# A depthwise convolution shared between VectorE and GpSimd: half the channels for each

## The reference

```python
def conformer_conv(a, g, conv_w, conv_b, ln_g, ln_b):
    z = a * jax.nn.sigmoid(g)                       # 256 tokens x 256 channels
    z = lax.conv_general_dilated(z, conv_w[:, None, :], window_strides=(1,),
                                 padding=[(D_CONV - 1, 0)],          # D_CONV = 31, causal
                                 dimension_numbers=('NWC', 'WIO', 'NWC'),
                                 feature_group_count=D_WIDTH) + conv_b
    return jax.nn.silu(layernorm(z, ln_g, ln_b))
```

## Time and profile before

| | |
|---|---|
| median of 3 runs | 1017.18 us (1016.47 to 1017.36) |
| the profiled execution | 1017.16 us, of which the span of the profile is 1015.3 us |
| busy: PE matmul, PE weight load | 1002.2 us (99%), 846.9 us (83%) |
| busy: DVE, ACT, POOL | 811.8 us (80%), 649.9 us (64%), 38.4 us (4%) |
| granted TensorE clock | full in all but the last instants |
| DMA | 257.13 MB, 253 GB/s over the span |

### The profile page before, as it was taken

One profiled execution on the slowest core, in us unless ns is written; L12 is line 12 of the kernel. 1 busy time (PEld: TensorE's weight loads), 2 busy tenths in 40 slices (PEclk: granted clock), 3 DMA queues, 4 the chain that ended last, 5 costly groups with the idle time before them and its releaser, 6 DMA issues.

```text
span 1015.3 us, 13999 instructions
## 1 busy us (share of the span) xinstructions
PE 1002.2 (99%) x4930; PEld 846.9 (83%) x4930; DVE 811.8 (80%) x1112; ACT 649.9 (64%) x890; POOL 38.4 (4%) x87
## 2 busy tenths in 40 slices
PE   7999999999999999999999999999999999999998
PEld 6888888888888888888888888888888988898887
DVE  5799888765544455699889768999889989989898
ACT  6658655555534443756674548787778787868775
POOL 6000000040000000100000000000000000000020
PEclk9999999999999999999999999999999999999999
DMA  9735555677555554844555556999999999999995
GB/s 272 240 122 168 172 179 168 209 241 248 169 195 188 195 177 129 289 147 133 178 172 181 189 190 217 323 379 389 365 340 393 384 364 346 390 369 362 358 395 204
DMA packets 117701, 257.13 MB, mean 253 GB/s; under 512 B 5217, under 2 KB 29859, under 8 KB 117649
## 3 DMA queue, kind: packets, MB, share of 16 engines
q1 hardware_dynamic: 113344, 243.55, 68.8%
q0 software_dynamic: 3296, 9.22, 3.3%
q10 hardware_dynamic: 1008, 3.67, 0.9%
HBM read 249.08 MB, written 7.34 MB: 253 GB/s over the span
## 4 chain that ended last, share of the span: by engine, by line
PE 89%; DVE 5%; ACT 3%; DMA 2%; issue 1%; SPq 0%; DVEq 0%; ACTq 0%
PE bank L390 27%; PE bank L392 27%; PE bank L391 27%; DMA ring<-in_w_in 2%; DVE wlo L378 1%; ACT whi L371 1%; PE bank L1082 1%; DVE dacc L1719 1%; PE bank L1005 1%; PE bank L1004 1%; PE bank L674 1%; DMA ring<-in_moe_w_gate 1%; PE bank L664 1%; PE bank L908 0%; PE bank L689 0%
## 5 line engine op out<-in xcount | busy, mean ns | idle before, releaser
L378 DVE TENSOR_TENSOR wlo<-ring,whi 128x1024 fp32r<-128x1024 f32 (+2 forms) x506 | 541.4, 1122 | 102.2 <-ACT whi L371 99.9
L371 ACT CAST whi<-ring 128x1024 fp32r<-128x1024 f32 (+2 forms) x506 | 463.4, 971 | 97.0 <-PE bank L392 79.1
L390 PE MATMUL bank<-whi,hTh 128*128 128x512 f32 (+3 forms) x992 | 375.4, 378 | 2.0 <-DVE wlo L378 1.3
L392 PE MATMUL bank<-whi,hTl 128*128 128x512 f32 (+3 forms) x992 | 370.4, 373 | 0.0
L391 PE MATMUL bank<-wlo,hTh 128*128 128x512 f32 (+3 forms) x992 | 370.1, 373 | 0.0
L390 PEld LDWEIGHTS bank<-whi,hTh 128*128 128x128 f32 x992 | 186.4, 188 | 32.4 <-issue 2.7
L392 PEld LDWEIGHTS bank<-whi,hTl 128*128 128x128 f32 x992 | 186.3, 188 | 29.1
L391 PEld LDWEIGHTS bank<-wlo,hTh 128*128 128x128 f32 x992 | 186.5, 188 | 28.4 <-issue 0.5
L390 PE MATMUL bank<-whi,oTh 128*128 128x512 f32 x392 | 155.4, 396 | 0.0
L392 PE MATMUL bank<-whi,oTl 128*128 128x512 f32 x392 | 153.1, 391 | 0.0
L391 PE MATMUL bank<-wlo,oTh 128*128 128x512 f32 x392 | 152.9, 390 | 0.0
(11 more groups left out here) (333 smaller groups left out, 672.4 us busy)
## 6 DMA issues: line engine op xcount, KB each, us to landing
ring<-in_w_in SPq DMA_DIRECT2D x40, 1024.0 KB, 5.2
ring<-in_moe_w_down SPq DMA_DIRECT2D x40, 1024.0 KB, 7.5
ring<-in_moe_w_gate SPq DMA_DIRECT2D x32, 1024.0 KB, 7.3
ring<-in_moe_w_up SPq DMA_DIRECT2D x32, 1024.0 KB, 8.2
ring<-in_moe_w_gate SPq DMA_DIRECT2D x16, 768.0 KB
ring<-in_moe_w_up SPq DMA_DIRECT2D x16, 768.0 KB, 7.4
ring<-in_ffn_w_gate SPq DMA_DIRECT2D x11, 1024.0 KB, 5.1
ring<-in_ffn_w_up SPq DMA_DIRECT2D x11, 1024.0 KB, 5.2
```

Source lines behind the costliest of these rows:

```text
L371: nc.scalar.copy(whi[pc.part(hf)][:, 0:n], pc.raw[:, hf * n:(hf + 1) * n]).then_inc(hi_done, 1)
L378: nc.vector.tensor_tensor(wlo[q][:, 0:n], pc.raw[:, hf * n:(hf + 1) * n], whi[q][:, 0:n].bitcast(F32), ALU.subtract).then_inc(lo_done, 1)
L390: nc.tensor.matmul(o, sh, wh, start=start, stop=False)
L392: return nc.tensor.matmul(o, sl, wh, start=False, stop=stop)
```

## The change

Of the two channel groups, group 1 moves to GpSimd. There each tap is two instructions, since the fused one isn't used: a product of the shifted view with the weight column into one of two temporaries (in `wsr`, which is free by then), and an addition to `dacc[:, 1]`. That is 1 + 30 x 2 = 61 instructions a layer. Each addition waits for its product and for the addition before. The call `conv(0)` stands behind `load_gain(1)` in GpSimd's program, `conv(1)` behind `load_gain(3)` and ahead of the filling of `yrows`.

DVE keeps group 0: 31 tap instructions a layer, each of which now waits for the one before (`link`). They are dealt anew to the steps: 4 in step 4, 4 in 6, 2 in 13, 3 in 14, 4 in 15, 5 in 16, 5 in 20, 4 in 22. After the last, DVE waits for `conv_done` from GpSimd and adds both groups.

```diff
+            def conv(l):
+                tmp = [wsr[:, 2 * i:2 * i + 2, :].rearrange("p g t -> p (g t)") for i in range(2)]
+                o, done = dacc[:, 1, :], (D_CONV - 1) * l
+                pool.wait_ge(zpad_ready, l + 1)
+                pool.wait_ge(wprep_ev, l + 1)
+                pool.wait_ge(param_in, 16 * N_PARAM * (l + 1))
+                nc.gpsimd.tensor_scalar(o, zpad[:, 1, 0:T], cw[:, 1, 0:1], dcol[:, 0, 1:2], ALU.mult,
+                                        ALU.add).then_inc(tap_sum, 1)
+                for j in range(1, D_CONV):
+                    nc.gpsimd.tensor_scalar(tmp[j % 2], zpad[:, 1, j:j + T], cw[:, 1, j:j + 1], None,
+                                            ALU.mult).then_inc(tap_product, 1)
+                    pool.wait_ge(tap_product, done + j)
+                    pool.wait_ge(tap_sum, D_CONV * l + j)
+                    nc.gpsimd.tensor_tensor(o, o, tmp[j % 2], ALU.add).then_inc(tap_sum, 1)
+                pool.wait_ge(tap_sum, D_CONV * (l + 1))
+                pool.engine_nop().then_inc(conv_done, 1)
...
             load_gain(1)
+            conv(0)
             pool.wait_ge(layer_done, 1)
             load_params(1)
             load_gain(2)
             load_gain(3)
+            conv(1)
...
-                for i in range(first, first + n):
-                    j, c = i // 2, i % 2
-                    if j:
-                        dve.wait_ge(dve_seq, own[0] - 1)
-                    z = zpad[:, c, j:j + T]
+                for j in range(first, first + n):
+                    z = zpad[:, 0, j:j + T]
                     if j == 0:
-                        ins = V.tensor_scalar(dacc[:, c, :], z, cw[:, c, 0:1], dcol[:, 0, c:c + 1], ALU.mult, ALU.add)
+                        ins = V.tensor_scalar(dacc[:, 0, :], z, cw[:, 0, 0:1], dcol[:, 0, 0:1], ALU.mult, ALU.add)
                     else:
-                        ins = V.scalar_tensor_tensor(out=dacc[:, c, :], in0=z, scalar=cw[:, c, j:j + 1],
-                                                     in1=dacc[:, c, :], op0=ALU.mult, op1=ALU.add)
-                    own[0] += 1
-                    ins.then_inc(dve_seq, 1)
-                if first + n == 2 * D_CONV:
-                    dve.wait_ge(dve_seq, own[0])
+                        ins = V.scalar_tensor_tensor(out=dacc[:, 0, :], in0=z, scalar=cw[:, 0, j:j + 1],
+                                                     in1=dacc[:, 0, :], op0=ALU.mult, op1=ALU.add)
+                    link(ins)
+                if first + n == D_CONV:
+                    dve.wait_ge(conv_done, l + 1)
                     V.tensor_tensor(dsum, dacc[:, 0, :], dacc[:, 1, :], ALU.add).then_inc(conv_ready, 1)
...
-                taps = {4: (0, 4), 5: (4, 10), 6: (14, 12), 13: (26, 4), 14: (30, 4), 16: (34, 8), 20: (42, 4),
-                        22: (46, 8), 23: (54, 8)}
+                taps = {4: (0, 4), 6: (4, 4), 13: (8, 2), 14: (10, 3), 15: (13, 4), 16: (17, 5), 20: (22, 5),
+                        22: (27, 4)}
```

More of the change, by code:

```diff
@@ L315, in build_trunk @@
         az_mm, az_ev = sem("az_mm"), sem("az_ev")
+        tap_product, tap_sum, conv_done = sem("tap_product"), sem("tap_sum"), sem("conv_done")
         conv_ready, dmean_mm, dsq_ready, dvar_mm, dms_root = (
```

## The result

| | before | changed |
|---|---|---|
| median | 1017.05 us (1016.47 to 1017.36) | 1031.9 us (1031.07 to 1032.86) |
| span of the profiled execution | 1015.3 us | 1030.0 us |

The ratio is 1.0146, with a 95% interval of 1.0134 to 1.0159: the changed kernel is 14.85 us slower. The prediction was 1029.5 us.

What follows compares the result with a forecast made beforehand. TensorE's matmuls, busy 1002.2 of 1015.3 us, were taken as the bound, with DVE a near second. Collisions of 6.8 us in layer 0 and 5.4 in layer 1, 12.2 together, gave 1029.4, predicted as 1029.5 us, range 1015.9 to 1043.

Steps and rivals of the forecast that it cites:

- What bounds the kernel, and what relief is worth: Whole program: TensorE's matmuls bound it; relief of DVE in both mixers gives back at most 1.74 us.
- The disputed term, exclusion: DVE instructions with two SBUF inputs wait for GpSimd instructions that read SBUF: 12.2 us in both layers, chance 58%.
- GpSimd's durations: GpSimd's taps: 0.25 us a product, 0.46 a sum, 0.65 upper bound of one; layer 0 done at about 93 us.
- p = 0.35 us a hit: Each two-input DVE instruction that meets a GpSimd one loses 0.35 us; 17 from piece 9's split to piece 11's first half.
- The spare that is taken off: At piece 9's split DVE can start only 1.3 us earlier in layer 0, 0.6 us in layer 1.
- The place: TensorE waits for DVE at piece 11, some 5 us in each layer, and nothing from 160 us on.
- a wait elsewhere: Sign against the prediction: TensorE's waits appear at places other than those it named.
- its sign for the collision: Splits longer than 1.2 us and rotations than 0.29 between 45 and 93 us and 429 and 480, as before outside.
- The sum: Both layers lose 12.2 us: layer 0 6.8 (4.7 to piece 11, 2.1 to piece 13), layer 1 5.4.
- GpSimd too slow for `conv_done`: DVE waits behind its last tap if a GpSimd instruction takes over 1.6 us; 1045 us at 2.0; chance 6%.
- no exclusion: The engines don't collide; TensorE loses its 0.61 us wait and little else, 0.8 us at most: 1016.4 us; chance 30%.
- the shed taps shorten the chain by 7 us: 18 taps fewer in steps 5 and 6 are worth 7 us by the chain: 1010 us; chance 6%.

Runs made afterwards that it cites:

- experiment 1: The changed kernel with GpSimd's 61 instructions a layer replaced by one memset, VectorE keeping its 31 taps: 1015.8 us, ratio 0.999.
- experiments 1 to 4: The changed kernel with GpSimd's taps replaced by one memset, by 61 memsets, by products only, by sums only: 1015.8, 1015.63, 1019.01, 1024.97 us.
- experiment 2: The changed kernel with all 61 GpSimd instructions a layer kept in place but made memsets of the same size: 1015.63 us, ratio 0.9986.
- experiments 3 and 4: The changed kernel with only GpSimd's product of each tap, then only its sum (unweighted): 1019.01 us (ratio 1.0019) and 1024.97 us (1.0081).
- experiment 7: The changed kernel with 8 and 11 small constant products on TensorE ahead of its two waits: 1029.78 us, ratio 1.0125.

## Why the prediction was right

The mechanism was right, the place and the sizes in part, and that the sum came near is luck.

- *What bounds the kernel, and what relief is worth* (at most 1.74 us, 0.8 likely): right, 1.0 us in experiment 1. The chain's 5.8% for the taps was no price, as argued.
- *The disputed term, exclusion*: right, shown by experiments 1 to 4. The Trainium skill's rule ("SBUF — State Buffer", Who interferes with whom) agrees with this trace in who collides: two SBUF inputs with GpSimd's reads (0.28 to 0.71 us), not with its writes (1.83 us for two splits in experiment 2), nor with one input in PSUM (1.94 us for four). It says that the loser waits for the whole instruction. In experiments 3 and 4 sums of 0.63 us or more hold VectorE's instructions for at most 0.58 us, and products of 0.92 us for at most 0.24; so by the measurement a product holds VectorE for about a quarter of its time at most.
- *GpSimd's durations* (0.25 and 0.46 us, extrapolated from memsets and selects): wrong by size, 0.92 and 0.72. Even the upper bound of 0.65 was too low. GpSimd was at work until 119.5 us, not 93.
- *p = 0.35 us a hit*: right in size for the sums, much too high for the products, and the count of hits was too high too. The predicted 17 x 0.35 = 6.0 us for the stretch from piece 9 to piece 11's first half was measured as 2.5 us, nine hits of 0.28 us on average (splits 0.18 + 0.07, scalings 0.53 + 0.69, rotations 1.06 us). The spare that is taken off was 1.7 us instead of 1.3 (piece 9's split starts at 58.78 us, before at 60.45), so of the predicted 4.7 us 0.9 were left: TensorE starts the rotated q and k at 75.46 us, before at 74.59.
- *The place*: half right. The wait came at the rotated q and k, one instruction ahead of piece 11, and grew by 1.4 us in layer 0; the prediction looked for some 5 us. The second wait, for the softmax at 104 us, wasn't in the sum: with GpSimd 26 us longer at work, the splits up to 105 us are hit as well. The prediction had named a wait elsewhere as a sign of being wrong; by this sign its account of place and length failed, while its sign for the collision (longer splits and rotations beside GpSimd, as before outside) came true.
- *The clock* wasn't in the sum either: 5.9 us at the lower clock in both layers, of which 2.1 came back in experiment 7.
- *The sum*, 12.2 us against 14.85: it came out near by luck. The hits up to piece 11 were priced and counted too high, and behind them the prediction has 2.1 us at piece 13, where the wait for the softmax and the clock came and took more; the two errors nearly cancel. Layer 1 was taken as cheaper than layer 0 (5.4 against 6.8 us); it loses as much, with waits of 2.2 and 2.5 us.
- *The rivals*: GpSimd too slow for `conv_done` didn't occur (1.22 us for each instruction against the limit of 1.6); no exclusion fell with the longer instructions of the changed kernel and with experiment 1; that the shed taps shorten the chain by 7 us fell with experiment 1, where they bring 1.0.

## What to carry to other kernels

Before you move elementwise work from VectorE to GpSimd, count VectorE's instructions with two SBUF inputs that will run beside it: here each one hit by a two-input instruction of GpSimd was some 0.4 us longer, so the moved work must be worth more than that and must hide where VectorE has slack. Ask first what relief of VectorE is worth at all, by the waits of the engine that bounds the kernel (here 1 us of 1017). If one wait is all there is, moving a few instructions of the late engine behind it is the cheaper cure.

## What was unexpected in the hardware

- GpSimd's product of 128x256 with a per-partition scalar took 0.92 us with one operation and 0.47 us with a second one added (times the weight, plus 0.0). The cause is open.
- A sum of GpSimd, the shorter instruction, holds VectorE more (18.3 us in all, +9.2 us of time, for 31 instructions a layer) than the longer product (4.7 and +3.2 us). That a second SBUF input on GpSimd's side is the reason fits both, but no kernel varied it alone.
- VectorE's scaling with one SBUF input is hit even by GpSimd's memsets (0.74 to 0.90 us for two), which leave its two-input instructions alone.
- GpSimd is held longer than VectorE in a collision: a product of 0.92 us took up to 2.96 us, while no instruction of VectorE was hit by more than 0.58 us.
- A product at half its time on GpSimd, whose work there ended 13 us earlier in layer 0, didn't make the kernel faster (1033.06 against 1031.9 us).
